# Hybrid decoder trunk on one core: another order of projection takes and threshold counts on ScalarE

## The chip, the cores and the metric

The kernel runs on one NeuronCore of a Trainium2 chip. It is written by hand, engine by engine, with semaphores between them: TensorE (PE) multiplies, VectorE (DVE), ScalarE (ACT) and GpSimd (POOL) compute elementwise, SyncE (SP) issues nearly all DMAs. The metric is the device time of one execution in microseconds.

## What is computed

Two layers over 1024 tokens of width 1024. Each normalises its rows, projects them with one weight matrix whose columns belong to four groups of heads (SSD, sparse attention DSA, latent attention MLA, forgetting attention FoX), joins the heads, projects back, and adds a mixture of experts. The change lies between the DSA group's index search and the projection of what MLA and FoX need later:

```python
proj = h @ w_in[l]
...
# dsa_mixer, for each block of 128 queries
rel = relu(einsum('bqjd,bkd->bqjk', qi_blk, k_idx))        # 8 index heads
score = einsum('bqjk,bqj->bqk', rel, wi_blk)
score = where(k_pos <= q_pos, score, -inf)
_, sel = top_k(score, 256)
k_sel, v_sel = k[sel], v[sel]
# softmax attention of the 4 heads over the 256 chosen keys
# mla_mixer, fox_mixer: full causal attention from other columns of proj
```

## The kernel before, in words

The stage in question is the joint stage, once per layer. It has two parts.

**Scoring.** The queries lie in eight tiles of 128; tiles 0 and 1 have at most 256 keys and need no choice. For tiles 7 down to 2, in 24 slots (a slot is one tile and one pair of index heads), TensorE forms the products (line 933), ScalarE takes their ReLU (`relu_pair`, line 1310), VectorE adds them up with their weights (lines 1747 and 1749).

**Search.** The 256th largest score of a row is found bit by bit: 31 trials, from bit 30 to bit 0, each a count of the scores that are not below a trial value. The tiles are shared out. Tile 7, the widest (1024 keys), has a search of its own: GpSimd forms its trial value (lines 630 and 631), ScalarE counts it (`widest_count`, a Sign activation with a sum, line 1318), GpSimd takes the result (lines 633 and 634). Sixteen of its 31 trials are counted in the scoring slots, the other 15 in the rounds. Tiles 2 to 6 are searched together, in 31 rounds n = 0 to 30: VectorE forms the trial values (`search_bit`: lines 1803 and 1805), counts tiles 2, 3 and 4 (line 1767) and takes all five results (lines 1797 and 1798); ScalarE counts tiles 6 and 5 (`pair_count`, 128x896 and 128x768, line 1318). ScalarE's pair of round n waits for VectorE's trial value, VectorE's lines 1797 and 1798 wait for the pair's counts. After round 30 VectorE closes the three wide tiles (`wide_end`: lines 1815, 1816, three counts at 1767), sets ones (line 1837), and the attention of DSA follows.

**Later projections.** Meanwhile TensorE computes 24 groups of the projection for MLA and FoX (`project_half`, lines 949 and 952): eight of 420 columns for MLA and the gates in the scoring slots, then eight of 128x512 for FoX's q and k (line 952), then eight of 128x256 for FoX's v (line 949). It has four PSUM banks for them, so a group waits until the fourth before it was taken out. ScalarE takes each out (`put_later(i)`, line 1343; for the first eight also line 1342) into a staging tile in SBUF, and SyncE stores it to DRAM (line 501) before the staging slot is used again. Takes 0 to 7 stand in scoring slots, takes 8 to 23 in the rounds. TensorE's order is its own and isn't touched: all 16 remaining groups one after the other, as banks come free.

Behind the last take stand SyncE's loads of what was stored and of MLA's weights (lines 507 to 513; their first late reader on ScalarE is line 1383, in the middle of the DSA attention), TensorE's first logits of the DSA attention (line 766), and a write of ones by GpSimd (line 646, 2 partitions of 8192 elements), which also stands behind GpSimd's own 31 trials. GpSimd has three shorter jobs between its trials (lines 637, 639, 641).

What sets the order of ScalarE's instructions is the Python loop below; its instructions run strictly in that order.

Of the kernel before, what the change touches and what calls it, by code (L numbers as in the profile page):

```python
# [75 lines left out]
def trunk(nc, x_in, positions, norm_mix, w_in, conv_w, conv_b, dt_bias, a_log, ssd_d, ssd_norm,  # L76
# [4 lines left out]
    with ctx:  # L81
# [220 lines left out]
        def uses(chunks):  # L302
            for c in chunks:
                for use in CHUNKS[c][1]:
                    for part in range(T if use[0] == "row" else 2):
                        yield c, use, part, use == CHUNKS[c][1][-1] and part == (T if use[0] == "row" else 2) - 1
# [380 lines left out]
        def _(pe):  # L687
# [24 lines left out]
            with pe.Fori(0, DEPTH) as l:  # L712
# [8 lines left out]
                def project(chunks, before=lambda n: None):  # L721
                    for c, use, part, last_use in uses(chunks):
                        before(proj.n)
                        n = proj.next()
                        if n >= 4:
                            pe.wait_ge(proj_taken, n - 3)
                        pe.wait_ge(w_loaded[c % 2], 16 * sum(len(CHUNKS[x][0]) for x in range(c % 2, c + 1, 2)))
                        kind, _, at, width = use
                        for k in range(K):
                            w = WR[:, c % 2, k, at:at + width]  # L730
                            if kind == "row":
                                m = pe.matmul(proj_bank(n)[:, 0:width], HT[:, k, part * P:(part + 1) * P], w,  # L732
                                              start=(k == 0), stop=(k == K - 1))
                            else:
                                m = pe.matmul(proj_bank(n)[0:width, :], w, HT[:, k, part * HALF:(part + 1) * HALF],  # L735
                                              start=(k == 0), stop=(k == K - 1))
                        m.then_inc(proj_ready, 1)
                        if last_use:
                            pe.wait_ge(proj_ready, n + 1)
                            pe.sem_inc(w_used, 1)  # L740
# [196 lines left out]
                def project_half(group, half):  # L937

                    c, use, part, last_use = later[group]
                    if half == 0:  # L940
                        n = proj.next()
                        pe.wait_ge(proj_taken, n - 3)
                        pe.wait_ge(w_loaded[c % 2], 16 * sum(len(CHUNKS[x][0]) for x in range(c % 2, c + 1, 2)))
                    n = proj.n - 1
                    kind, _, at, width = use
                    for k in range(4 * half, 4 * half + 4):
                        w = WR[:, c % 2, k, at:at + width]
                        if kind == "row":
                            m = pe.matmul(later_bank(n)[:, 0:width], HT[:, k, part * P:(part + 1) * P], w,  # L949
                                          start=(k == 0), stop=(k == K - 1))  # L950
                        else:
                            m = pe.matmul(later_bank(n)[0:width, :], w, HT[:, k, part * HALF:(part + 1) * HALF],  # L952
                                          start=(k == 0), stop=(k == K - 1))
                    if half == 1:
                        m.then_inc(proj_ready, 1)
                        if last_use:
                            pe.wait_ge(proj_ready, n + 1)
                            pe.sem_inc(w_used, 1)
# [165 lines left out]
        def _(act):  # L1124
# [45 lines left out]
            with act.Fori(0, DEPTH) as l:  # L1170
# [127 lines left out]
                later = list(uses(LATER_CHUNKS))  # L1298
                trials = Ring()
# [21 lines left out]
                def widest_count():  # L1321
                    n = trials.next() + 1
                    sign_count(WIDE[0], trial_ready, trial_counted, n)
                    act.wait_ge(trial_counted, n)

                def pair_count(n):
                    for i, t in enumerate(WIDE[1:]):
                        sign_count(t, pair_trial, pair_counted, n + 1)
                        act.wait_ge(pair_counted, 2 * n + i + 1)

                def put_later(i):

                    _, use, part, _ = later[i]
                    n = proj.next()
                    name, width = use[1], use[3] if use[0] == "row" else HALF
                    act.wait_ge(proj_ready, n + 1)
                    if i >= 4:
                        act.wait_ge(stage_out[i % 4], 16 * (i // 4))
                    scale = HD ** -0.5 if name in (("foxqk", 0), ("foxqk", 1)) else 1.0
                    if name == "mla":  # L1340
                        width = 416
                        act.activation(f_rows[:, part, :], later_bank(n)[:, 416:420], ACT.Copy)
                    act.activation(stage[:, i % 4, 0:width], later_bank(n)[:, 0:width], ACT.Copy,
                                   scale=scale).then_inc(proj_taken, 1)
# [7 lines left out]
                i = N_HALVES // 2  # L1352
                for n in range(31):
                    pair_count(n)
                    if n % 2 == 0 and trials.n < 31:
                        widest_count()
                    if i < len(later) and n >= 1:
                        put_later(i)
                        i += 1
                assert trials.n == 31  # L1360
# [44 lines left out]
                for t in range(T):  # L1405
                    n = proj.next()
# [4 lines left out]
                    n = proj.next()  # L1411
# [718 lines left out]
```

## Time and profile before

| what | us |
|---|---|
| median of three runs | 2938.73 |
| lowest, highest | 2933.47, 2940.27 |
| the profiled execution, own time | 2944.05 |
| its span in the trace | 2942.3 |
| joint stage, rounds, layer 1 | 446.3 to 574.3 |
| joint stage, rounds, layer 2 | 1894.1 to 2021.9 |

The times are device times of whole executions. The profile is of one further execution; its span is a little shorter than its time, and times in the trace count from the span's start. Busy time is the time in which an engine executes something; idle time stands in brackets behind the instruction that follows it, with what released it. The granted clock is a share of TensorE's 2.4 GHz: 0.50 is the lower level of 1.2 GHz, 1.00 the upper.

### The profile page before, as it was taken

How to read it: one execution, taken by the hardware profiler on the slowest of the kernel's cores; microseconds unless marked ns; L12 is line 12 of the kernel's file. 1: busy time of each engine (PE TensorE's matmuls, PEld its weight loads, DVE VectorE, ACT ScalarE, POOL GpSimd, SP SyncE). 2: the span in 40 equal slices, each digit the busy share in tenths (PEclk: the TensorE clock that was granted, in tenths of full speed). 3: DMA queues.
4: the chain of work that ended last, by engine and by line, in shares of the span. 5: the costliest groups of instructions: out<-in, count | busy, mean ns of one | idle time of the engine just before them, and what ended most of it. 6: DMA issues, size and time to landing. Idle time of an engine off the chain costs nothing.

```text
span 2942.3 us, 30451 instructions
## 1 busy us (share of the span) xinstructions
PE 2503.1 (85%) x10356; PEld 1423.7 (48%) x10374; DVE 1228.1 (42%) x2854; ACT 908.3 (31%) x1878; POOL 195.6 (7%) x372
## 2 busy tenths in 40 slices
PE   5979999188999959999579899973889997899994
PEld 3464445155664635454335644451556645445452
DVE  4342266885551331111332514768755414211115
ACT  2131266654450201111112214765544401111112
POOL 0000021200000000000200000211000000100002
PEclk9989999599999979999779899996999997899996
DMA  6100011301000369999411001121010005699985
GB/s 222 40 29 24 32 35 38 95 2 44 1 1 9 121 254 362 369 361 371 167 59 49 7 24 38 40 81 41 2 44 1 10 22 208 243 357 371 364 305 193
DMA packets 105455, 370.44 MB, mean 126 GB/s; under 512 B 20754, under 2 KB 39912, under 8 KB 80744
## 3 DMA queue, kind: packets, MB, share of 16 engines
q1 hardware_dynamic: 91500, 318.41, 30.2%
q0 software_dynamic: 13824, 50.34, 4.5%
q8 instruction: 76, 1.25, 0.2%
q14 instruction: 55, 0.45, 0.1%
HBM read 304.42 MB, written 64.30 MB: 125 GB/s over the span
## 4 chain that ended last, share of the span: by engine, by line
PE 75%; DVE 13%; ACT 5%; issue 4%; DMA 1%; POOL 0%; ACTq 0%; DVEq 0%; SPq 0%; POOLq 0%
PE bank L1065 15%; PE bank L732 9%; PE bank L1082 8%; PE bank L1013 8%; PE bank L735 6%; PE bank L766 6%; PE bank L696 5%; PE bank L949 4%; PE bank L952 4%; PE bank L795 4%; PE bank L933 2%; ACT group_arena L1318 2%; PE bank L1026 1%; PE bank L1051 1%; DVE residual L2090 1%
## 5 line engine op out<-in xcount | busy, mean ns | idle before, releaser
L696 PE MATMUL bank<-ident,group_arena 128*128 128x128 f32 (+1 forms) x1200 | 201.1, 308 | 129.1 <-DVE group_arena L1537 59.8
L766 PE MATMUL bank<-group_arena 96*128 96x512 f32 (+7 forms) x384 | 165.7, 531 | 133.9 <-ACTq L1216 125.9
L732 PE MATMUL bank<-w_ring,normed_cols 128*128 128x260 f32 (+2 forms) x768 | 268.0, 511 | 0.6 <-PE bank L735 0.6
L696 PEld LDWEIGHTS bank<-ident,group_arena 128*128 128x128 f32 (+1 forms) x1200 | 149.8, 156 | 190.0 <-issue 96.1
L1082 PE MATMUL bank<-heads_cols,group_arena 128*128 128x512 f32 x512 | 231.8, 595 | 2.8 <-DVE group_arena L2050 2.8
L1065 PE MATMUL bank<-w_ring,group_arena 128*128 128x512 f32 x512 | 229.5, 602 | 3.3 <-issue 1.7
L1065 PE MATMUL bank<-normed_cols,group_arena 128*128 128x512 f32 x512 | 224.9, 592 | 0.0
L1013 PE MATMUL bank<-w_ring,heads_cols 128*128 128x512 f32 x512 | 222.6, 594 | 2.0 <-DVEq L251 2.0
L732 PEld LDWEIGHTS bank<-w_ring,normed_cols 128*128 128x128 f32 x768 | 147.0, 192 | 120.0 <-issue 112.6
L1604 DVE TENSOR_REDUCE softmax_stats<-bank 128x1 f32<-128x128 f32 (+7 forms) x192 | 145.5, 758 | 122.7 <-PE bank L771 105.6
L2050 DVE COPY group_arena<-bank 128x256 f32<-128x256 f32 x64 | 27.2, 425 | 395.3 <-PE bank L1072 395.3
L735 PE MATMUL bank<-normed_cols,w_ring 128*128 128x512 f32 x384 | 170.1, 604 | 15.1 <-DMA w_ring<-in_w_in 14.5
L653 POOL DMA_INDIRECT group_arena<-h_rows,group_arena x64 | 60.4, 944 | 1586.1 <-DVEq L2038 973.0
L1065 PEld LDWEIGHTS bank<-w_ring,group_arena 128*128 128x128 f32 x512 | 98.6, 193 | 127.6 <-issue 125.6
L1065 PEld LDWEIGHTS bank<-normed_cols,group_arena 128*128 128x128 f32 x512 | 97.3, 190 | 122.5 <-issue 122.5
L949 PE MATMUL bank<-w_ring,normed_cols 128*128 128x420 f32 (+1 forms) x512 | 154.5, 454 | 0.6 <-PE bank L952 0.6
L1013 PEld LDWEIGHTS bank<-w_ring,heads_cols 128*128 128x128 f32 x512 | 96.3, 190 | 119.1 <-issue 116.7
L766 PEld LDWEIGHTS bank<-group_arena 128*128 128x128 f32 (+1 forms) x384 | 69.6, 211 | 170.3 <-ACTq L1216 125.7
L1440 ACT ACTIVATE group_arena<-bank 128x256 f32<-128x256 f32 x64 | 24.6, 385 | 406.6 <-PE bank L1065 406.6
L1318 ACT ACTIVATE group_arena<-heads_cols,group_arena 128x896 bf16<-128x896 f32 (+1 forms) x124 | 135.6, 1093 | 41.8 <-DVEq L1806 34.1
L1767 DVE TENSOR_SCALAR_CACHE_REDUCE group_arena<-group_arena 128x384 bf16<-128x384 f32 (+3 forms) x200 | 141.4, 755 | 12.1 <-DVE group_arena L1805 11.0
L1082 PEld LDWEIGHTS bank<-heads_cols,group_arena 128*128 128x128 f32 x512 | 92.2, 190 | 95.4 <-issue 91.8
(326 smaller groups left out, 3479.8 us busy)
## 6 DMA issues: line engine op xcount, KB each, us to landing
heads_cols<-in_expert_w_down SPq DMA_DIRECT2D x64, 1024.0 KB, 9.0
w_ring<-in_expert_w_gate SPq DMA_DIRECT2D x32, 1024.0 KB, 10.0
w_ring<-in_expert_w_up SPq DMA_DIRECT2D x32, 1024.0 KB, 14.5
normed_cols<-in_expert_w_gate SPq DMA_DIRECT2D x32, 1024.0 KB, 10.5
normed_cols<-in_expert_w_up SPq DMA_DIRECT2D x32, 1024.0 KB, 15.1
expert_rows<-group_arena SPq DMA_DIRECT2D x64, 512.0 KB, 9.2
w_ring<-in_w_in SPq DMA_DIRECT2D x6, 2048.0 KB, 8.3
expert_rows<-heads_cols SPq DMA_DIRECT2D x1, 8192.0 KB, 28.7
```

The source lines that it names most:

```text
L696: last = pe.transpose(bank(4 + r % 2)[0:rows, col:col + src.shape[0]], src, ident[0:src.shape[0], 0:src.shape[0]])
L732: m = pe.matmul(proj_bank(n)[:, 0:width], HT[:, k, part * P:(part + 1) * P], w, start=(k == 0), stop=(k == K - 1))
L735: m = pe.matmul(proj_bank(n)[0:width, :], w, HT[:, k, part * HALF:(part + 1) * HALF], start=(k == 0), stop=(k == K - 1))
L766: m = pe.matmul(L[:, c0:c1], a["q"](h, t), a["k"](h, c0, c1), start=True, stop=not (by_choice or diagonal))
L795: pe.matmul(O[i * HD:(i + 1) * HD, pair * P:(pair + 1) * P], KINDS[kind]["v"](h + i, b), pT[:, (u + i) % 2, b * P:(b + 1) * P], start=(b = ...
L949: m = pe.matmul(later_bank(n)[:, 0:width], HT[:, k, part * P:(part + 1) * P], w, start=(k == 0), stop=(k == K - 1))
L1013: m = pe.matmul(bank(n % 4)[:, :], YT[:, k, t * P:(t + 1) * P], WR[:, slot, k, :], start=(k == 0), stop=(k == K - 1))
L1065: m = pe.matmul(bank(2 + s)[:, :], xgT[:, s, k, :], Wgu[w][:, :, k, :], start=(k == 0), stop=(k == K - 1))
L1082: m = pe.matmul(bank(6 + h)[:, :], aT[:, s, k, :], Wd[w][:, k, h * HALF:(h + 1) * HALF], start=(k == 0), stop=(k == 1))
L1318: act.activation(sign_junk[:, 0:w], flipped[t], ACT.Sign, bias=trial_bias[:, t - 2:t - 1], scale=SIGN_SCALE, accum_out=thr[:, 0, t - 2:t - ...
L1604: chain(dve.tensor_reduce(st_[:, u % 4, 0:1], PS[n % 2][:, 0:(t + 1) * P], AX_X, ALU.max))
L1767: chain.go(dve.tensor_scalar(to, src(t), limit(t), 0.0, ALU.is_ge, ALU.add, accum_out=thr[:, 0, t - 2:t - 1]))
```

## The change

In the rounds, the widest tile's counts move from the even to the odd rounds. The takes of groups 8 to 23 move from rounds 1 to 16 to the even rounds 2 to 16 (groups 8 to 15) and to every round from 18 to 25 (groups 16 to 23). Both kernels have 15 widest counts and 16 takes in the rounds.

```diff
                 for n in range(31):
                     pair_count(n)
-                    if n % 2 == 0 and trials.n < 31:
+                    if n % 2 == 1 and trials.n < 31:
                         widest_count()
-                    if i < len(later) and n >= 1:
+                    if i < len(later) and (n >= 18 or n >= 2 and n % 2 == 0):
                         put_later(i)
                         i += 1
```

Only ScalarE's order changes; those of TensorE, VectorE, GpSimd and SyncE are the same, row by row. In the rows below 128x896 and 128x768 are the pair's counts of a round, 128x1024 is the widest tile's count, line 1343 a take. First ScalarE at the start of the rounds, before the change, rounds 0 to 2:

```order
L1318 ACTIVATE group_arena<-heads_cols,group_arena 128x896
L1318 ACTIVATE group_arena<-group_arena 128x768
L1318 ACTIVATE group_arena<-heads_cols,group_arena 128x1024
L1318 ACTIVATE group_arena<-heads_cols,group_arena 128x896
L1318 ACTIVATE group_arena<-group_arena 128x768
L1343 ACTIVATE heads_cols<-bank 128x512
L1318 ACTIVATE group_arena<-heads_cols,group_arena 128x896
L1318 ACTIVATE group_arena<-group_arena 128x768
L1318 ACTIVATE group_arena<-heads_cols,group_arena 128x1024
L1343 ACTIVATE heads_cols<-bank 128x512
```

And after the change, rounds 0 to 2 and the pair and the count of round 3:

```order
L1318 ACTIVATE group_arena<-heads_cols,group_arena 128x896
L1318 ACTIVATE group_arena<-group_arena 128x768
L1318 ACTIVATE group_arena<-heads_cols,group_arena 128x896
L1318 ACTIVATE group_arena<-group_arena 128x768
L1318 ACTIVATE group_arena<-heads_cols,group_arena 128x1024
L1318 ACTIVATE group_arena<-heads_cols,group_arena 128x896
L1318 ACTIVATE group_arena<-group_arena 128x768
L1343 ACTIVATE heads_cols<-bank 128x512
L1318 ACTIVATE group_arena<-heads_cols,group_arena 128x896
L1318 ACTIVATE group_arena<-group_arena 128x768
L1318 ACTIVATE group_arena<-heads_cols,group_arena 128x1024
```

The take of the first group comes a round later, and a round has either the widest tile's count or a take, no longer both or a take in every round.

The end of the rounds on ScalarE, before the change, rounds 28 to 30:

```order
L1318 ACTIVATE group_arena<-heads_cols,group_arena 128x896
L1318 ACTIVATE group_arena<-group_arena 128x768
L1318 ACTIVATE group_arena<-heads_cols,group_arena 128x1024
L1318 ACTIVATE group_arena<-heads_cols,group_arena 128x896
L1318 ACTIVATE group_arena<-group_arena 128x768
L1318 ACTIVATE group_arena<-heads_cols,group_arena 128x896
L1318 ACTIVATE group_arena<-group_arena 128x768
L1212 ACT_TABLE_LOAD
```

And after it:

```order
L1318 ACTIVATE group_arena<-heads_cols,group_arena 128x896
L1318 ACTIVATE group_arena<-group_arena 128x768
L1318 ACTIVATE group_arena<-heads_cols,group_arena 128x896
L1318 ACTIVATE group_arena<-group_arena 128x768
L1318 ACTIVATE group_arena<-heads_cols,group_arena 128x1024
L1318 ACTIVATE group_arena<-heads_cols,group_arena 128x896
L1318 ACTIVATE group_arena<-group_arena 128x768
L1212 ACT_TABLE_LOAD
```

The last count of the widest tile stands in round 29 instead of 28, so one round less lies between it and the end.

## Rows read from the trace of the kernel before

**Rows 1.** The page, busy time, share of the span and instructions of two engines.

```profile
PE 2503.1 (85%) x10356; PEld 1423.7 (48%) x10374; DVE 1228.1 (42%) x2854; ACT 908.3 (31%) x1878; POOL 195.6 (7%) x372
```

**Rows 2.** The chain of waits, in order of time: start us, us, what; layer 1's rounds.

```profile
438.37 56.22 PE bank L952 x128
...
566.94 5.04 DVE group_arena L1805
```

**Rows 3.** ScalarE's waits from 446.2 to 523: us in total, times, longest us.

```profile
ACT heads_cols L1343 <- issue: 19.7, 7, 4.2
```

**Rows 4.** TensorE's timeline, layer 1: start us, us, line, what, count [idle before].

```profile
494.88 27.86 PE L949 MATMUL bank<-w_ring,normed_cols 128*128 128x256 f32 x128 [0.30 <-PE bank L952]
```

**Rows 5.** ScalarE's timeline, layer 1: the takes of two q/k groups one after the other.

```profile
487.80 0.60 ACT L1343 ACTIVATE heads_cols<-bank 128x512 f32<-128x512 f32 x1 [4.19 <-issue]
...
494.66 0.60 ACT L1343 ACTIVATE heads_cols<-bank 128x512 f32<-128x512 f32 x1 [2.92 <-issue]
```

**Rows 6.** ScalarE's timeline, layer 1: the starts of rounds 18, 19 and 20.

```profile
526.73 1.04 ACT L1318 ACTIVATE group_arena<-heads_cols,group_arena 128x896 bf16<-128x896 f32 x1 [1.03 <-DVEq L1806]
...
530.23 1.04 ACT L1318 ACTIVATE group_arena<-heads_cols,group_arena 128x896 bf16<-128x896 f32 x1
...
533.45 1.04 ACT L1318 ACTIVATE group_arena<-heads_cols,group_arena 128x896 bf16<-128x896 f32 x1 [1.03 <-DVEq L1806]
```

**Rows 7.** ScalarE's timeline, layer 1: the starts of rounds 10, 11 and 12.

```profile
498.94 1.03 ACT L1318 ACTIVATE group_arena<-heads_cols,group_arena 128x896 bf16<-128x896 f32 x1
...
502.71 1.03 ACT L1318 ACTIVATE group_arena<-heads_cols,group_arena 128x896 bf16<-128x896 f32 x1
...
505.86 1.04 ACT L1318 ACTIVATE group_arena<-heads_cols,group_arena 128x896 bf16<-128x896 f32 x1
```

**Rows 8.** ScalarE's timeline: starts of rounds 0, 28, 30, its end; layer 2's 0, 30.

```profile
446.26 1.04 ACT L1318 ACTIVATE group_arena<-heads_cols,group_arena 128x896 bf16<-128x896 f32 x1 [4.41 <-DVEq L1806]
...
560.54 1.04 ACT L1318 ACTIVATE group_arena<-heads_cols,group_arena 128x896 bf16<-128x896 f32 x1 [1.23 <-DVEq L1806]
...
572.12 1.04 ACT L1318 ACTIVATE group_arena<-heads_cols,group_arena 128x896 bf16<-128x896 f32 x1 [5.89 <-DVEq L1806]
...
574.13 0.19 ACT L1318 ACTIVATION_READ_ACCUMULATOR group_arena<-group_arena 128x1 f32 x1
...
1894.09 1.04 ACT L1318 ACTIVATE group_arena<-heads_cols,group_arena 128x896 bf16<-128x896 f32 x1 [4.41 <-DVEq L1806]
...
2019.72 1.04 ACT L1318 ACTIVATE group_arena<-heads_cols,group_arena 128x896 bf16<-128x896 f32 x1 [5.90 <-DVEq L1806]
```

**Rows 9.** Timelines of GpSimd (first row) and VectorE at the end of the rounds, layer 1.

```profile
565.02 6.92 POOL L646 MEMSET normed_cols<- 2x8192 f32 x1 [0.15 <-POOL group_arena L634]
...
566.54 0.17 DVE L1798 COPY_PREDICATED group_arena<-group_arena 128x5 int32<-128x5 int32 x1
...
566.94 5.03 DVE L1805 TENSOR_SCALAR group_arena<-group_arena 128x2 f32<-128x2 f32 x1
...
574.82 0.17 DVE L1815 COPY group_arena<-group_arena 128x3 f32<-128x3 f32 x1
...
579.92 0.91 DVE L1837 MEMSET group_arena<- 128x1024 f32 x1 [0.28 <-DVE group_arena L1835]
```

**Rows 10.** Windows, TensorE: stretch, length, busy (instructions), granted clock, DMA share, GB/s.

```profile
425.00:438.00 13.00, 8.32 (x26) 0.70 0.32 97
437.00:440.00 3.00, 3.00 (x8) 0.50 0.00 0
494.90:522.80 27.90, 27.84 (x128) 1.00 0.13 43
```

**Rows 11.** Line 1383's summary (ns, first and last start); DMA issues, us to landing.

```profile
L1383 ACT ACTIVATE group_arena<-group_arena x16: 416/417/421, 637.1 to 2108.7; 128x256 f32<-128x256 f32 x16
...
group_arena<-latent_rows SPq DMA_DIRECT2D x2, 1664.0 KB, 21.1
```

## The prediction

> **What bounds the kernel now.** I read the page first, then the chain of waits, then ScalarE's waits and timeline in the joint stage. By busy time TensorE leads with 85% of the span against 31% for ScalarE [rows 1]; that is an average over stages and says nothing of this one. The chain tells it [rows 2]: in layer 1 it lies on TensorE's projection from 438.4 us on, 56.2 us at line 952 alone, and afterwards no longer on TensorE but on the rounds; the long piece there is one VectorE instruction of 5.0 us at line 1805. So the 31 search rounds have two parts. While projection groups are left, a round waits for a group: ScalarE stood 19.7 us before line 1343 for a bank that wasn't full [rows 3]. Once they are gone it waits for VectorE's next trial, 1.03 us in a round without the widest tile's count [rows 6] and 5.89 us once, before round 30 [rows 8].
>
> The sizes: eight fox q/k groups take TensorE 56.2 us, eight fox v groups 27.86 us, back to back from 438.4 to 494.88 + 27.86 = 522.7 [rows 2, 4]. Before the change a group is taken in every round 1 to 16, so a q/k round lasts as long as a q/k group, 494.66 - 487.80 = 6.86 us [rows 5], though ScalarE has only about 4 us of work in it. A pair of rounds with no group at all takes 533.45 - 526.73 = 6.72 us, of which 530.23 - 526.73 = 3.50 with the widest tile's count and 3.22 without [rows 6]. A pair of v rounds, each with a group and one with the count, takes 505.86 - 498.94 = 6.92 us, 3.77 with the count and 3.15 without [rows 7].
>
> **The change, part by part.** Nothing is added or removed on any engine: ScalarE's 31 pair counts, 15 widest counts and 16 takes remain. Two things move: the widest count from even to odd rounds, and the takes from rounds 1 to 16 to the even rounds 2 to 16 (q/k) and rounds 18 to 25 (v).
>
> *Rounds 0 to 17.* Now one q/k group is due per two rounds. A round without the count ends in ScalarE's wait for the next trial, 1.03 us long [rows 6]; the take of 0.60 us [rows 5] goes into that wait, and the v rounds show it fits (3.15 us with a take, 3.22 with none [rows 6, 7]). So a pair costs 6.72 us, and nine pairs 60.5 us.
> Does TensorE keep up? It starts at 438.4, 8 us before round 0 [rows 2, 8], has four banks, and finishes a group per 6.87 us; counted back from the take at 494.66 [rows 5], which had waited for the eighth, the first is out at about 446.6. The take of group j (j = 0 to 7) would come at 446.26 + 6.72 (j+1) + 2.2 = 455.2 + 6.72 j, the group is ready at 446.6 + 6.87 j: 8.6 us of slack at the first and 7.5 at the last. The bank for group j+4 comes free at about 455.8 + 6.72 j, and TensorE asks for it at 467.2 + 6.87 j. So neither waits for the other, and the pace is that of ScalarE and VectorE.
>
> *Rounds 18 to 25.* Every round takes a v group, every second has the count: the pattern of rows 7, four pairs of 6.93, 27.7 us (before, the same rounds had no group: 4 x 6.72 = 26.9). A v group costs TensorE 27.86 / 8 = 3.48 us against a round of 3.46, and by then four are in the banks; it stands still for about 0.6 and 0.9 us before its fifth and sixth v group and is done at about 524.3, hardly later than before.
>
> *Rounds 26 to 29.* Two pairs, 13.4 us.
> The start of round 30 is thus 60.5 + 27.7 + 13.4 = 101.6 us after that of round 0. Before it was 572.12 - 446.26 = 125.9 in layer 1 and 2019.72 - 1894.09 = 125.6 in layer 2 [rows 8]. Gain: 24.2 and 24.0 us, 48.2 together. Some 5 us of each is the stall of the next paragraph, which leaves this place.
>
> *The stall at the end.* When its last count is in, GpSimd writes 2x8192 elements at line 646, 6.92 us from 565.02; VectorE's line 1805, 0.17 us otherwise, took 5.03 us and ended with it [rows 9]. Now the last widest count is in round 29. The memset came 565.02 - 560.54 = 4.48 us after the start of its round [rows 8, 9]; round 29 starts 3.50 us before round 30, so it runs from 1.0 to 7.9 us after the start of round 30. Line 1805 of that round has passed by then: ScalarE's pair waits for it. The pair count ends 574.32 - 572.12 = 2.20 us into the round [rows 8], and VectorE reaches the copy of line 1815 at 574.82 - 572.12 = 2.7 us [rows 8, 9], in the middle of the memset. This trace has no COPY during it. Bounds: nothing (line 1798, under the memset, took its usual 0.17 us [rows 9]; a copy of 3 elements may behave like it) and 7.9 - 2.7 = 5.2 us, less the 0.17 it takes anyway. I take 5.1: the nearest row is line 1805, like the copy one tensor of float32 from SBUF to SBUF of two or three elements. By the Trainium skill (SBUF — State Buffer, Who interferes with whom) a VectorE copy or tensor_scalar in a two-port mode is blocked for the whole of a GpSimd instruction; by VectorE: DVE Perf Modes, What auto-detection actually checks, a copy enters that mode if the outer dimensions of source and destination are even or equal, and 3 equals 3. By that rule the stall stays, and no run here shows it for an odd size.
> Cost: 5.1 us per layer, 10.2 together.
>
> *Others at nothing.* The shorter GpSimd writes and the copy between the trials follow the widest count as before and fall into VectorE's counts as before. SyncE's loads behind the last take start some 12 us later, at about 535. Their first reader that can suffer is line 1383, at 637.1, some 18 us earlier after the change; the load takes 21.1 us to land [rows 11]. The others follow it in the queue with far less to move. That leaves some 60 us. If this cover were gone, each us late would be a us lost. The first logits of the attention need the last take (about 535) but their first softmax comes after 555: covered too. TensorE is idle before the attention in both kernels and starts it at the low clock.
>
> **Sum.** -48.2 + 10.2 = -38.0 us. The profiled execution took 2944.05 us by its own time, so 2906.0 for it; it stands 5.3 us above the median shown, so the forecast for the median is 2938.73 - 38.0 = 2900.7 us.
>
> **Rivals.**
> *The stall goes away.* If line 1815 isn't blocked, VectorE works on to its own memset at line 1837, 579.92 - 574.82 = 5.1 us further [rows 9], when GpSimd is done. Then -48.2 us: 2890.5. For it: line 1798, of five elements, wasn't held up, and no row has a copy of an odd size. Against: the row of line 1805 [rows 9].
>
> *The clock falls in the late v groups.* TensorE now has short gaps in rounds 18 to 21. At the end of scoring, where it was busy for 8.32 of 13 us, the granted clock did come down to 0.50, the lower level of 1.2 GHz; in unbroken projection it was at 1.00, 2.4 GHz [rows 10]. If the last four v groups ran at the low level, 7 us each from 509.4 on, the takes of rounds 24 and 25 would wait 0.7 and 2.3 us: 3 us per layer, -32, 2906.7. Against: in scoring TensorE stood still for a third of the time, here for 1.5 us in fifteen.
>
> *Slower.* TensorE at 1.2 GHz from its fifth group on. The 522.7 - 467.2 = 55.5 us that are left would take 111, to 578.3; the last take would end round 25 at 579.0, round 30's pair would end at 594.6, and with the stall moved behind it the stage would be 594.6 + 5.1 - 574.3 = 25.4 us longer, 51 in all: 2989.5. It decides the sign once more than some 30 us of the projection's work runs at the low level. The Trainium skill (TensorE: Matmul & The Clock Gate, What's actually happening) has the clock follow how busy the engine has been, which speaks against a change that spreads its work. Against it here: up to 509 us the work isn't spread, since TensorE has a free bank at every group's end, and unbroken work ran at 1.00 [rows 10].
>
> *Nothing happens.* The order of the built program has moved as the code says, so only a bound that I don't see, such as a wait of takes on their stores, could give 2939. Before, the v groups' stores went out at one per 3.5 us and no take waited for one.
>
> **How the numbers follow.** The forecast has 0.65, the vanished stall 0.24, the low clock in late groups 0.06, slower 0.03, nothing 0.02. The range reaches from 2888 (2890.5 less 2.5 of scatter; the three runs span 6.8 us) to 2909 (2906.7 and 2.3). 0.2% is 5.9 us, about what a measurement can tell here: faster 0.96, same 0.01, slower 0.03.
>
> **What would show it.** Right: round 30's pair starts about 101.6 us after round 0's in both layers; takes of q/k groups 6.7 us apart with no wait for TensorE; v rounds alternate 3.8 and 3.15 us; line 1805 never over 0.2 us; line 1815 about 5.2 us long; projection back to back at a clock of 1.00 to about 509. Wrong: a wait for a group at line 1343, a granted clock of 0.50 before 520, line 1815 at 0.17 us (then 2890), or a pair of rounds above 6.9 us before round 18. The forecast would also fail if the attention behind the stage, which I leave as it is, became longer by some us.

## The result and the profile after

| | us |
|---|---|
| before, median of four runs | 2939.5 (2933.47 to 2941.52) |
| after, median of four runs | 2898.71 (2897.82 to 2899.95) |
| after over before | 0.9865, 95% interval 0.9848 to 0.9882 |
| the profiled execution after, own time and span | 2897.82 and 2896.1 |

The changed kernel is 40.8 us faster; the forecast was 38.0, that is 2900.7 us. The page's busy times have hardly moved, so the gain is waiting, not work. These are the page's rows of the kernel after, the span and the busy times:

```profile
span 2896.1 us, 30469 instructions
...
PE 2498.8 (86%) x10374; PEld 1419.4 (49%) x10374; DVE 1228.4 (42%) x2854; ACT 910.0 (31%) x1878; POOL 196.0 (7%) x372
```

The chain of waits in the rounds of layer 1 (start us, us, what) no longer has the projection's 56 us of [rows 2]; one v group of 3.7 us is left of it, which by ScalarE's waits below no take waited for, and the stall, VectorE's wait for GpSimd's write of ones, stands at line 1815 instead of 1805:

```profile
508.59 3.73 PE bank L949 x16
512.87 1.13 ACT group_arena L1318 x2
539.10 1.25 ACT group_arena L1318 x2
549.80 5.23 DVE group_arena L1815
```

ScalarE's waits from 445.8 to 560 (us in total, times, longest): the 19.7 us at line 1343 of [rows 3] are gone, only the wait for the next trial is there.

```profile
ACT group_arena L1318 <- DVEq L1806: 12.5, 16, 4.4
```

ScalarE's timeline gives the starts of the rounds: 0, 2, the first take and round 3, round 4; then rounds 18 to 20 with their takes; then 26 and 30; last, rounds 0 and 30 of layer 2.

```profile
445.86 1.04 ACT L1318 ACTIVATE group_arena<-heads_cols,group_arena 128x896 bf16<-128x896 f32 x1 [4.40 <-DVEq L1806]
...
452.58 1.04 ACT L1318 ACTIVATE group_arena<-heads_cols,group_arena 128x896 bf16<-128x896 f32 x1
454.81 0.60 ACT L1343 ACTIVATE heads_cols<-bank 128x512 f32<-128x512 f32 x1
455.74 1.04 ACT L1318 ACTIVATE group_arena<-heads_cols,group_arena 128x896 bf16<-128x896 f32 x1 [0.34 <-DVEq L1806]
459.24 1.04 ACT L1318 ACTIVATE group_arena<-heads_cols,group_arena 128x896 bf16<-128x896 f32 x1
...
505.93 1.04 ACT L1318 ACTIVATE group_arena<-heads_cols,group_arena 128x896 bf16<-128x896 f32 x1
508.15 0.38 ACT L1343 ACTIVATE heads_cols<-bank 128x256 f32<-128x256 f32 x1
509.09 1.04 ACT L1318 ACTIVATE group_arena<-heads_cols,group_arena 128x896 bf16<-128x896 f32 x1 [0.56 <-DVEq L1806]
512.59 0.38 ACT L1343 ACTIVATE heads_cols<-bank 128x256 f32<-128x256 f32 x1
512.87 1.03 ACT L1318 ACTIVATE group_arena<-heads_cols,group_arena 128x896 bf16<-128x896 f32 x1
...
533.67 1.03 ACT L1318 ACTIVATE group_arena<-heads_cols,group_arena 128x896 bf16<-128x896 f32 x1
...
547.10 1.04 ACT L1318 ACTIVATE group_arena<-heads_cols,group_arena 128x896 bf16<-128x896 f32 x1
...
1872.48 1.04 ACT L1318 ACTIVATE group_arena<-heads_cols,group_arena 128x896 bf16<-128x896 f32 x1 [4.41 <-DVEq L1806]
...
1973.81 1.04 ACT L1318 ACTIVATE group_arena<-heads_cols,group_arena 128x896 bf16<-128x896 f32 x1
```

No take waits for its group. The wait for the next trial is 0.34 us behind a q/k take, since the take now fills most of the 1.03. A pair of rounds with a q/k take is 459.24 - 452.58 = 6.66 us, a v pair 512.87 - 505.93 = 6.94. Round 0 to round 30 takes 547.10 - 445.86 = 101.2 us and 1973.81 - 1872.48 = 101.3 in layer 2, against 125.9 and 125.6 [rows 8].

GpSimd's write and VectorE's copy, the timelines of the kernel after at the end of layer 1's rounds (first row GpSimd, the others VectorE), answer to [rows 9]:

```profile
548.08 6.92 POOL L646 MEMSET normed_cols<- 2x8192 f32 x1 [0.15 <-POOL group_arena L634]
...
549.60 0.17 DVE L1798 COPY_PREDICATED group_arena<-group_arena 128x5 int32<-128x5 int32 x1
549.80 5.22 DVE L1815 COPY group_arena<-group_arena 128x3 f32<-128x3 f32 x1
...
559.95 0.91 DVE L1837 MEMSET group_arena<- 128x1024 f32 x1 [0.28 <-DVE group_arena L1835]
```

TensorE, windows of the kernel after (stretch, length, busy, granted clock, DMA share, GB/s): the clock stays at 1.00, its level of 2.4 GHz, through the late v groups with their short pauses.

```profile
494.40:512.30 17.90, 17.76 (x80) 1.00 0.10 38
512.30:524.00 11.70, 10.67 (x49) 1.00 0.13 45
```

From round 0 to line 1837 layer 1 went from 579.92 - 446.26 = 133.7 us to 559.95 - 445.86 = 114.1.

### The profile page after: what moved, and what is told of

It is laid out like the page before. It is cut to its first block, busy times and chain, and to the rows that moved or that the text cites. A ratio compares the mean times of both kernels' runs of the same rounds, so it can differ in the third digit from the quotient of the medians.

```text
span 2896.1 us, 30469 instructions
## 1 busy us (share of the span) xinstructions
PE 2498.8 (86%) x10374; PEld 1419.4 (49%) x10374; DVE 1228.4 (42%) x2854; ACT 910.0 (31%) x1878; POOL 196.0 (7%) x372
## 3 DMA queue, kind: packets, MB, share of 16 engines
q8 instruction: 76, 1.25, 0.2%
## 4 chain that ended last, share of the span: by engine, by line
PE 71%; DVE 15%; issue 6%; ACT 6%; DMA 1%; POOL 0%; DVEq 0%; ACTq 0%; SPq 0%; POOLq 0%
PE bank L1065 15%; PE bank L732 9%; PE bank L1082 8%; PE bank L1013 8%; PE bank L735 6%; PE bank L766 5%; PE bank L696 5%; PE bank L795 4%; PE bank L949 3%; ACT group_arena L1318 2%; PE bank L933 1%; DVE residual L2090 1%; PE bank L1026 1%; PE bank L1051 1%; DVE group_arena L1537 1%
## 5 line engine op out<-in xcount | busy, mean ns | idle before, releaser
L1318 ACT ACTIVATE group_arena<-heads_cols,group_arena 128x1024 bf16<-128x1024 f32 (+1 forms) x124 | 135.7, 1094 | 33.0 <-DVEq L1806 25.0
## 6 DMA issues: line engine op xcount, KB each, us to landing
normed_cols<-in_expert_w_gate SPq DMA_DIRECT2D x32, 1024.0 KB, 10.2
```

The lines of the kernel that those rows point to most:

```text
L1318: act.activation(sign_junk[:, 0:w], flipped[t], ACT.Sign, bias=trial_bias[:, t - 2:t - 1], scale=SIGN_SCALE, accum_out=thr[:, 0, t - 2:t - ...
```

## Experiments

Each kernel was timed beside the kernel before. In the table, "rounds" is from the start of round 0's pair to that of round 30 on ScalarE, layer 1, and "to 1837" from the same point to VectorE's line 1837.

| kernel | us | over before, 95% | rounds | to 1837 | line 1805, longest | line 1815 |
|---|---|---|---|---|---|---|
| before | 2939.5 | | 125.9 | 133.7 | 5.03 | 0.17 |
| after | 2898.7 | 0.9848 to 0.9882 | 101.2 | 114.1 | 0.17 | 5.22 |
| takes alone | 2910.9 | 0.9881 to 0.9914 | 110.6 | 118.4 | 5.02 | 0.17 |
| counts alone | 2940.3 | 0.999 to 1.0009 | 120.7 | 133.6 | 0.17 | 5.22 |
| after, ones by DMA | 2890.5 | 0.9812 to 0.9845 | 101.2 | 109.0 | 0.17 | 0.17 |
| before, ones by DMA | 2930.3 | 0.9952 to 0.998 | 120.9 | 128.7 | 0.17 | 0.17 |
| after, 1815 in another form | 2891.0 | 0.9819 to 0.9852 | 101.2 | 109.0 | 0.17 | 0.16 |
| takes in all even rounds | 2899.1 | 0.9847 to 0.988 | 99.9 | 114.5 | 0.17 | 6.91 |
| the same, ones by DMA | 2886.7 | 0.9803 to 0.9836 | 100.0 | 107.8 | 0.17 | 0.17 |
| takes in rounds 15 to 30 | 2905.1 | 0.9866 to 0.9899 | 109.9 | 117.7 | 0.17 | 0.17 |

The kernel before had a median of 2940.3 beside the first four experiments and of 2938.8 beside the last four.

### One part of the change at a time

The takes' new places with the counts as before:

```diff
-                    if n % 2 == 1 and trials.n < 31:
+                    if n % 2 == 0 and trials.n < 31:
```

> The changed kernel, but with the widest tile's counts left in the even rounds, so that rounds 2, 4 .. 16 hold a count and a q/k take both. My theory: TensorE no longer bounds, the round with both costs about 3.99 us and the empty one 3.22, 7.2 a pair instead of 6.7, and the stall stands before round 30 again. Round 0 to round 30: 6.7 + 8 x 7.2 + 27.7 + 13.4 + 4.9 = 110.4 us, line 1805 once at 5.0 us, line 1815 at 0.17 us, time about 2898.7 + 8 = 2907. Rival (only the thinner demand for groups matters, the place of the count doesn't): 106.3 us, time 2899.

Measured: 110.6 us of rounds against 110.4 expected, and 2910.9 us against 2907. ScalarE's timeline of this kernel shows a round with a count and a take, round 2, and the wait of 1.03 us that comes back behind round 3:

```profile
454.31 1.04 ACT L1318 ACTIVATE group_arena<-heads_cols,group_arena 128x896 bf16<-128x896 f32 x1 [1.03 <-DVEq L1806]
...
456.54 1.15 ACT L1318 ACTIVATE group_arena<-heads_cols,group_arena 128x1024 bf16<-128x1024 f32 x1
457.59 0.19 ACT L1318 ACTIVATION_READ_ACCUMULATOR group_arena<-heads_cols,group_arena 128x1 f32 x1
457.81 0.60 ACT L1343 ACTIVATE heads_cols<-bank 128x512 f32<-128x512 f32 x1
458.30 1.03 ACT L1318 ACTIVATE group_arena<-heads_cols,group_arena 128x896 bf16<-128x896 f32 x1
...
461.51 1.04 ACT L1318 ACTIVATE group_arena<-heads_cols,group_arena 128x896 bf16<-128x896 f32 x1 [1.03 <-DVEq L1806]
```

461.51 - 454.31 = 7.20 us for the pair, 0.54 more than in the changed kernel. Up to line 1837 it is 4.3 us per layer slower than the changed kernel, 8.6 in all; the medians differ by 12.2, so 3.5 us of that lie outside the stage. In its profiled execution (2914.2 us), the part of layer 2 from 200 us behind line 1837 to the attention's end took 116.0 us at a lower granted clock, against 109.1 us at 1.00 in the changed kernel:

```profile
2196.42:2312.44 116.02, 108.67 (x879) 0.94 0.00 1
```

Its four runs fall into two pairs, 2907.0 and 2909.0 us with a mean granted clock of 0.930, 2912.7 and 2914.2 with 0.926. Such a stretch can account for the difference, but only one run of it has a trace, so that isn't shown. The rival that the count's place doesn't matter is out.

The counts' new places with the takes as before:

```diff
-                    if n % 2 == 0 and trials.n < 31:
+                    if n % 2 == 1 and trials.n < 31:
```

> The kernel before, but with the widest tile's counts in the odd rounds; takes as before in rounds 1 to 16. My theory: rounds 5 to 16 are paced by TensorE's groups (6.87 and 3.48 us), so nothing is gained there; only the stall moves from line 1805 to line 1815. Round 0 to round 30 about 121.0 us (125.9 less 4.9), line 1815 at 5.2 us, time 2939 within 3 us. Rival (the count's place has a share of the gain of its own): up to 4 us per layer, 2931.

Measured: no difference (interval 0.999 to 1.0009), 120.7 us of rounds, the stall at line 1815. ScalarE's waits of this kernel from 447.9 to 525 us show that TensorE paces it as before:

```profile
ACT heads_cols L1343 <- issue: 18.4, 5, 4.2
ACT group_arena L1318 <- DVEq L1806: 5.8, 3, 4.4
```

So the spread of the takes carries the gain, and the counts' place is worth about 4 us a layer on top of it and nothing without it.

### The stall

GpSimd's write of ones at line 646 is left out and a DMA of the same ones put on SyncE's queue, in the changed kernel and in the kernel before:

```diff
-                pool.wait_ge(proj_taken, sum(1 for _ in uses(SSD_CHUNKS + DSA_CHUNKS + LATER_CHUNKS)))
-                pool.memset(HT[64:66, :, :], 1.0).then_inc(fox_fixed, 1)
...
+                sp.dma_start(HT[64:66, :, :].rearrange("p k (c n) -> p (k c) n", n=P),
+                             ones[64:66, :].unsqueeze(1).to_broadcast([2, K * SEQ // P, P])).then_inc(fox_fixed, 16)
                 sp.dma_start(HT[0:HD, :, :], fox_qk_dram.rearrange("(h d) s -> d h s", d=HD)).then_inc(fox_in, 16)
...
-                sp.wait_ge(fox_fixed, 1)
+                sp.wait_ge(fox_fixed, 16)
```

> The changed kernel, but the ones that GpSimd wrote at line 646 come by a DMA on SyncE's queue, before the load of q and k. My theory: line 1815 waited for GpSimd's write and for nothing else, so it takes 0.17 us and each layer is 5.06 us shorter: 2898.7 - 10.1 = 2888.6. Rival (the 5.2 us are a wait for something else that comes at that time, such as the search's end on GpSimd, or the next VectorE work waits instead): 2898.7, with line 1815 or the line behind it still late.

> The kernel before, with the same DMA instead of GpSimd's write at line 646. My theory: line 1805 is never over 0.2 us, each layer 4.9 us shorter: 2939.5 - 9.8 = 2929.7, and the stall is worth the same in both kernels. Rival as for the changed kernel: 2939.5.

Measured: 8.2 us less than the changed kernel by the medians and 5.1 per layer up to line 1837; 10.1 less than the kernel before beside it, 4.9 in layer 1. Line 1815 in the changed kernel with the DMA, and line 1805 in the kernel before with it (how many; shortest, median and longest in ns; first and last start):

```profile
L1815 DVE COPY group_arena<-group_arena x2: 169/169/169, 550.2 to 1973.7; 128x3 f32<-128x3 f32 x2
```

```profile
L1805 DVE TENSOR_SCALAR group_arena<-group_arena x62: 168/169/170, 445.7 to 2010.5; 128x2 f32<-128x2 f32 x62
```

So the stall was GpSimd's write and nothing else, and up to line 1837 it cost about the same in both kernels. That the changed kernel gained 8.2 us and not 10.2 by its median (2890.5, 2888.6 expected) lies behind the stage: in the profiles of both variants of the changed kernel without the stall, the way from line 1837 to the attention's end is 310.7 us in each layer, with the stall 309.0. Why was not tried.

Then the write stays, and one VectorE instruction gets another form:

```diff
-                    chain(dve.tensor_copy(want, real_want[:, cols]))
+                    chain(dve.scalar_tensor_tensor(want, real_want[:, cols], 0.0, real_want[:, cols], ALU.mult, ALU.add))
```

> The changed kernel with one instruction written in another form: line 1815's copy of 3 elements becomes a scalar_tensor_tensor with two tensor inputs and the same result. GpSimd's write stays. My theory: what is held up is the form that reads one SBUF tensor (TENSOR_SCALAR, COPY), not the moment; the new form passes as lines 1797 and 1798 do, VectorE goes on under the write and reaches line 1837 about 5.1 us later, when GpSimd is done: 5.0 us per layer, 2889 to 2891, as with the DMA. Rival (the next instructions are held up in its place: line 1816 or the counts): 2898.7, a row of 5 us at one of these lines.

Measured: 2891.0 us, the same 109.0 us to line 1837 as with the DMA. The timelines of this kernel (GpSimd, then VectorE) have the write running from 550.20 to 557.12 with VectorE working on under it:

```profile
550.20 6.92 POOL L646 MEMSET normed_cols<- 2x8192 f32 x1 [0.15 <-POOL group_arena L634]
...
551.92 0.16 DVE L1815 SCALAR_TENSOR_TENSOR group_arena<-group_arena 128x3 f32<-128x3 f32 x1
552.12 0.16 DVE L1816 CUSTOM_DVE_ANT_0 group_arena<-bits,group_arena 128x6 uint16<-128x6 uint16 x1
552.40 1.01 DVE L1767 TENSOR_SCALAR_CACHE_REDUCE group_arena<-group_arena 128x768 bf16<-128x768 f32 x1
```

So at this moment the form of the instruction decides.

### Where the takes stand

```diff
-                    if i < len(later) and (n >= 18 or n >= 2 and n % 2 == 0):
+                    if i < len(later) and n % 2 == 0:
```

> The changed kernel with every take in an even round, 0 to 30, so that no round has both a count and a take. Round 0 to round 30: 15 x 6.72 = 100.8 us instead of 101.2. The last take is in round 30, so GpSimd's write starts with VectorE's line 1815 at about the same time, within 0.1 us: if the copy is first, the write runs under the counts and line 1815 takes 0.17 us, with at most 1 us of stall later at line 1605 (2890); if the write is first, line 1815 waits all 6.9 us (2902). TensorE has a v group of 3.5 us per 6.7 us of rounds from round 16 on; if its granted clock falls to 0.50 there, that costs nothing, since four groups are in the banks. Rival: the clock falls and the takes wait, rounds 16 to 30 above 3.5 us each.

Measured: 2899.1 us, where 2902 was expected for the case that the write comes first. The rounds are shorter than I expected, 99.9 us: a take in a round without a count costs nothing and even saves 0.06 us (6.66 a pair against 6.72 with none). What the rounds gain on the changed kernel, 1.3 us, is given back at the end. GpSimd's write, which waits for the last take, began 0.04 us before VectorE's copy, as these two timelines of the kernel show (VectorE, then GpSimd), and the copy waited for all of it:

```profile
550.55 6.91 DVE L1815 COPY group_arena<-group_arena 128x3 f32<-128x3 f32 x1
...
550.51 6.92 POOL L646 MEMSET normed_cols<- 2x8192 f32 x1 [1.84 <-ACT heads_cols L1343]
```

TensorE runs ahead of the takes and has one long pause, 2.94 us before its last v group. The clock, at 1.00 up to 524 us, was at 0.50 from 525 to 527 and back at 1.00 from 528, and that group took 5.41 us instead of 3.48; it was done at 529.3 and taken only at 550.1, and no take waited, so the rival is out. TensorE's timeline of the last group, and its windows around it:

```profile
523.87 5.41 PE L949 MATMUL bank<-w_ring,normed_cols 128*128 128x256 f32 x16 [2.94 <-ACT heads_cols L1343]
```

```profile
510.00:520.00 10.00, 10.00 (x48) 1.00 0.08 26
520.00:530.00 10.00, 6.33 (x21) 0.83 0.04 14
530.00:540.00 10.00, 0.00 (x0) 0.71 0.08 26
```

The same order of takes together with the DMA of ones:

> The same order of takes with the ones by DMA. My theory: 0.4 us per layer less than the changed kernel with the DMA (100.8 instead of 101.2 us from round 0 to 30), no stall; 2889.6 against 2890.5, which only the rounds' own times can show. Rival: the later last take makes the first logits or the loads late, and VectorE waits at line 1604 behind line 1837: 2891 to 2895.

Measured: 2886.7 us, 100.0 us of rounds, no stall, 107.8 us to line 1837; this is 1.25 us in layer 1 better than the changed kernel with the DMA, not 0.4, for the reason just given. It is the fastest kernel here, 52 us below the one before and 12 below the changed one. The late last take cost nothing that shows: line 1383 begins 56.2 us behind line 1837, in the changed kernel 56.5.

Last, all takes pressed into the second half of the rounds:

```diff
-                    if i < len(later) and (n >= 18 or n >= 2 and n % 2 == 0):
+                    if i < len(later) and n >= 15:
```

> The changed kernel with the 16 takes in rounds 15 to 30, one in each, so that TensorE stands still from about 466 to 500 us and has 12 groups to do in rounds 15 to 30. A test of the low clock. My theory: the granted clock falls to 0.50 in the pause and is back at 1.00 within the first group (it costs about 1.5 us, as at 438), then the rounds are paced by TensorE again: last group at about 557, round 0 to round 30 about 108 us, the stall at line 1815 gone and 1.6 us of it at line 1605: 3.5 us per layer above the changed kernel, 2906. Rival (unsteady work keeps the clock low): 12 groups in 110 us, round 0 to 30 about 163 us, above 2999.

Measured: 2905.1 us (2906 expected), 109.9 us of rounds (108 expected). The total came out by luck: the rounds were 1.9 us longer than expected, and the 1.6 us of stall expected at line 1605 were not there. TensorE's timeline and windows of this kernel show the pause and the groups after it:

```profile
502.54 30.03 PE L952 MATMUL bank<-normed_cols,w_ring 128*128 128x512 f32 x64 [33.58 <-ACT heads_cols L1343]
```

```profile
475.00:498.00 23.00, 0.00 (x0) 0.50 0.00 0
498.00:502.00 4.00, 0.00 (x0) 0.50 0.00 0
502.00:506.00 4.00, 3.46 (x4) 0.50 0.17 66
506.00:520.00 14.00, 14.00 (x33) 0.96 0.20 76
520.00:557.00 37.00, 36.70 (x142) 1.00 0.12 43
```

The clock was at 0.50, 1.2 GHz, after the pause and back at the upper level within the first q/k group: four of them took 30.03 us, and at full clock they would take 4 x 6.87 = 27.5, so the pause cost 2.5 us of clock, not 110 us of slow groups. One expectation failed: line 1605, of one element, took its usual 0.15 us under the write. The next TENSOR_SCALAR of many elements was held up, for 0.2 us: it took 0.61 us, 0.42 in the changed kernel. VectorE's timeline of this kernel, the write ending at 568.19:

```profile
567.08 0.15 DVE L1605 TENSOR_SCALAR softmax_stats<-softmax_stats 128x1 f32<-128x1 f32 x1
...
567.80 0.61 DVE L1847 TENSOR_SCALAR group_arena<-group_arena 128x384 f32<-128x384 f32 x1
```

## Why the prediction was right

**What bounds the rounds.** Right. The chain and ScalarE's waits had named TensorE's groups, and the removed 19.7 us of waits reappear nowhere. The experiment that leaves the takes in rounds 1 to 16 gains nothing; the one that spreads them gains some 70% of the whole (29.5 of 40.8 us).

**Rounds 0 to 17.** Expected 60.5 us, measured 505.93 - 445.86 = 60.1. The 0.4 us are the pairs with a take, 6.66 instead of 6.72: the row of a v round with a take had shown 3.15 us against 3.22, and I took the larger.

**Rounds 18 to 25 and 26 to 29.** 27.7 expected, 533.67 - 505.93 = 27.7 measured; 13.4 and 13.4.

**The stall at the end.** Right, 5.2 us at line 1815, from 1.0 to 7.9 us after round 30's start (548.08 - 547.10 = 1.0). By the rule of the Trainium skill that the prediction cites (SBUF — State Buffer, Who interferes with whom; VectorE: DVE Perf Modes, What auto-detection actually checks), a copy of 3 elements stays blocked; the runs agree with 5.22 and 6.91 us, and the same result computed with two tensor inputs passed in 0.16. The rival with the stall gone would have been right had the copy been of another form. Its price up to line 1837, 5.1 and 4.9 us per layer, was measured in both kernels.

**Others at nothing.** Right as far as they show: line 1383 begins 56.5 us behind line 1837 (57.2 before), and 56.2 with the last take in round 30 and the ones by DMA, so no load was late there; no first logits were late either.

**The low clock.** Neither rival came. Pauses of at most 0.72 us between v groups left the granted clock at 1.00. A pause of 33.6 us, in the run with late takes, brought it down to 0.50, and it came back with the work; it cost 2.5 us per layer, where a slower result would have needed some 30 us of work at the low level. This agrees with the Trainium skill (TensorE: Matmul & The Clock Gate, What's actually happening), by which the clock follows how busy the engine has been.

**The size.** The stage gave 19.6 us in layer 1 and, from 2027.53 - 1894.09 = 133.4 to 1986.67 - 1872.48 = 114.2, 19.3 in layer 2: 38.8 of the 40.8. Between the two profiled executions the rest is larger, since their spans differ by 46.2 us. Most of it is the FoX attention of layer 2, which neither kernel's edit touches. The windows from 200 us behind line 1837 to the attention's end (before, then after) are 114.5 and 109.1 us long, the former with a lower granted clock:

```profile
2227.50:2342.00 114.50, 107.16 (x870) 0.94 0.00 1
```

```profile
2186.70:2295.80 109.10, 100.86 (x866) 1.00 0.00 1
```

Layer 1 of the kernel before had 110.0 us at a clock of 1.00 for the same part. In layer 2 the two other kernels with the takes in rounds 1 to 16 had 109.8 (counts alone) and 109.6 us (ones by DMA), and the one with takes alone, which has the new places, had 116.0. So the places of the takes don't make it. What is left is 2.0 us: 0.4 before round 0 of layer 1, where no edit reaches and the ten profiles lie between 445.9 and 448.5, and 1.6 between line 1837 of layer 1 and round 0 of layer 2 (1314.2 and 1312.5 us, in the other profiles 1312.0 to 1315.0). That is within what profiles differ by elsewhere. The medians too leave 2 us outside the stage, and nothing here says where they lie.

## What to carry to other kernels

An engine with few instructions of its own can still be the pace of a stage through the place where its results are taken: look at what the taking engine waits for in each round, and spread the takes so that groups are due no faster than the computing engine finishes them. Put the small work of a round where the engine already waits for another, here 0.6 us of take into 1.03 us of wait, and not behind work that fills that wait. And when a transfer of ones or zeros to two partitions runs on GpSimd, see which VectorE instruction meets it; a DMA, or another form of one three-element copy, was worth 8 to 10 us here.

## What I had not expected of the hardware

A VectorE COPY of 3 elements waited for GpSimd's write to its end (5.22 us, and 6.91 where the write began 0.04 us ahead of it), and so did a TENSOR_SCALAR of 2 elements (5.03). One of 384 elements, begun 0.39 us before the write's end, took 0.61 us instead of 0.42, while a TENSOR_SCALAR of one element took 0.15 us under the same write, and SCALAR_TENSOR_TENSOR, COPY_PREDICATED and the counts with their sums went on as usual. And a take in a round without a count made the pair of rounds 0.06 us shorter than no take at all.
